# Encoder trunk: eight weight slots around norms, the last FFN step by token block, block 0 turned at other places, loads reordered at the start

## The chip, the cores and the metric

The kernel runs on one core of a Trainium2 chip. The metric is the device time of one execution in microseconds (us), taken as the median of several runs.

## The reference, cut to what matters

Two layers (`DEPTH = 2`) work on one sequence of 256 tokens with 1024 features, in fp32. `memory_cross_attention` reads 256 rows of a second input, `mem`.

```python
for l in range(DEPTH):
    x = layer_norm(ALPHA * x + 0.5 * swiglu(x, ffn1_w13[l], ffn1_w2[l]), ln_g[l, 0], ln_b[l, 0])
    h = x @ w_in[l]                                # pool channels | c_q | c_kv | k_pe
    y_mix = jnp.concatenate([pool_mixer(...), mla_mixer(...)], axis=-1) @ w_out[l]
    x = layer_norm(ALPHA * x + y_mix, ln_g[l, 1], ln_b[l, 1])
    y_mem = memory_cross_attention(x, mem, mem_wq[l], mem_wkv[l], mem_wo[l])
    x = layer_norm(ALPHA * x + y_mem, ln_g[l, 2], ln_b[l, 2])
    x = layer_norm(ALPHA * x + 0.5 * swiglu(x, ffn2_w13[l], ffn2_w2[l]), ln_g[l, 3], ln_b[l, 3])
```

`swiglu` is `(silu(x @ gate) * (x @ up)) @ w2` with an inner width of 2816.

## The kernel before

**Arithmetic.** Every matrix product is made of three fp32r matmuls: high part by high part, high by low, low by high. So every weight must be split before it is used: ScalarE casts it to the high part (L985), VectorE subtracts to get the low part (L1168). The same is done with activations.

**Weights as units.** Weights come as 366 units of 128 x 1024 (512 KB), in one fixed order. SyncE loads unit n into one of four raw buffers once VectorE has split unit n-4 (L479). ScalarE and VectorE then write it into one of six slots (`slot_hi`, `slot_lo`); a slot is free again when TensorE has passed the last matmul that reads it. A `Plan` counts TensorE's milestones ahead of time, and a table (`slot`, `last_user`, `free_after`) says which slot each unit takes. ScalarE and VectorE are in-order engines: the splits of coming units are put between their other work by `ahead(tag)`, which splits as many units as will have free slots when TensorE reaches that milestone, and by `ahead_to(n)`.

**FFN.** 11 steps (`FS`), of which 8 run in a hardware loop of 4 iterations x 2 steps. A step multiplies four units against both blocks of 128 tokens (`up`, 48 matmuls), turns the hidden values of the step before in the middle of that (`turn_hidden`, L698), and multiplies two units into the output rows (`down`, 24 matmuls). ScalarE makes the silu (L1025) and the cast of the turned values (L1030), VectorE the product with the up half (L1216) and the low part (L1221). At the end block 0's output is finished first (milestone `("y", e, 0)`), then block 1's in two halves of 512 columns (`("half y", e)`, `("y", e, 1)`).

**Norms.** There are eight, e = 0 to 7: e % 4 = 0 after the first FFN, 1 after `w_out`, 2 after the memory read, 3 after the second FFN. The last, e = 7, ends the kernel. VectorE does block 0 first: two halves of sum and statistics (L1258, L1261), variance (L1265, L1267), centre (L1272), then the scaling (L1280) after GpSimd's power (L1473); after that the same for block 1, with the splits of coming units in between. TensorE then turns the normed block (L613) in two halves, ScalarE casts it (L1018), and VectorE makes its low part (L1206); only then can the next stage read it. To have work in that time, TensorE computes one 256-column piece of the memory's keys or values (a *fill*, two units, 48 matmuls of 256 columns). Table `FILL` has one for every norm except those after the memory read and the second FFN of layer 1. After e = 0 and e = 1 block 1 is turned after the fill; after e = 2 and e = 3 it is turned inside the next FFN's first step, `up_begin`, which runs all of block 0 (24 matmuls) before block 1.

**The start.** SyncE issues in this order: identity, x block 0, x block 1, units 0 to 2, the other constants, unit 3, `mem` (1 MB), unit 4 and so on. TensorE turns x block 0, runs three units of `up_begin` for block 0, turns block 1, and turns `mem` between FFN steps 0 and 1. GpSimd computes the rope angles at once when constants and positions are there.

Names that the change touches: `SLOTS`, `STEPS`, `plan_norm`, `plan_rows`, `plan_ffn`, the slot table, `load`, `column_pair`, `fill`, `second_block`, `up_begin`, `turn_hidden`, `ahead`, `gate`, `round_hidden`, `multiply`, `split_hidden`, `norm`.

## Time and profile before

| | us |
|---|---|
| median of 3 runs (1176.31 to 1177.42) | 1177.41 |
| the profiled execution, its own time | 1177.25 |
| its span, first to last instruction | 1175.5 |

```profile
span 1175.5 us, 16505 instructions
```

The span is what the trace covers; 1.75 us lie around it. In the trace, PE is TensorE's matmuls, PEld its weight loads, DVE VectorE, ACT ScalarE, POOL GpSimd, SPq the queue that issues DMAs. L535 is the line of all matmuls of products, so stages are told apart by tiles and times.

### The profile page before, as it was taken

What the parts mean: (1) busy time and instruction counts of PE and PEld (TensorE: products, weight loads), DVE (VectorE), ACT (ScalarE), POOL (GpSimd) and SP (SyncE); (2) the same over time, 40 slices, a digit from 0 to 9 for tenths busy, and PEclk for the clock granted to TensorE, in tenths of its full rate; (3) what the DMA queues carried; (4) which work ended last, traced back from release to release, by engine and by line L of the source; (5) the groups of instructions that cost most, each with busy time, mean ns of one, the idle gap of its engine ahead of it and who ended that gap; (6) DMA issues with size and microseconds to landing.
All of it is one profiled execution on the core that took longest, in us unless ns stands there. A gap on an engine that the chain in (4) does not pass through costs nothing.

```text
span 1175.5 us, 16505 instructions
## 1 busy us (share of the span) xinstructions
PE 1123.4 (96%) x6020; PEld 968.4 (82%) x6020; DVE 717.6 (61%) x856; ACT 511.7 (44%) x670; POOL 106.1 (9%) x116
## 2 busy tenths in 40 slices
PE   5999999999999999999999999999999998999996
PEld 4888888899899888888888888879888986888884
DVE  3655555878766765555585555567768757555555
ACT  3544444346355254444444444434553524444440
POOL 5800000150100100000010000001401000000001
PEclk9999999999999999999999999999899998999998
DMA  8655666434482486666556665544335527665650
GB/s 257 208 185 181 194 192 196 140 117 157 126 268 93 126 267 189 186 182 194 162 183 211 194 188 188 181 141 144 121 111 190 185 88 221 200 188 183 192 161 36
DMA packets 162802, 203.56 MB, mean 173 GB/s; under 512 B 16928, under 2 KB 144160, under 8 KB 162752
## 3 DMA queue, kind: packets, MB, share of 16 engines
q1 hardware_dynamic: 159824, 194.22, 52.9%
q0 software_dynamic: 2928, 8.66, 2.3%
q8 instruction: 33, 0.54, 0.2%
q14 instruction: 17, 0.14, 0.0%
HBM read 201.79 MB, written 1.05 MB: 173 GB/s over the span
## 4 chain that ended last, share of the span: by engine, by line
PE 88%; DVE 7%; POOL 1%; ACT 1%; issue 1%; DMA 1%; SPq 0%; POOLq 0%; DVEq 0%
PE ps L535 84%; PE ps L698 2%; DVE st L1261 1%; DVE x L1258 1%; POOL st L1473 1%; DVE x L1280 1%; PE ps L613 1%; DVE w_lo L1168 1%; DMA raw<-in_ffn_w 1%; DVE xT L1206 0%; POOL tmp L1535 0%; DVE x L1272 0%; PE ps L796 0%; DVE v_flat L1168 0%; DVE xT L1180 0%
## 5 line engine op out<-in xcount | busy, mean ns | idle before, releaser
L1168 DVE TENSOR_TENSOR w_lo<-raw,w_hi 128x1024 fp32r<-128x1024 f32 (+2 forms) x253 | 306.9, 1221 | 170.9 <-ACT w_hi L985 170.2
L985 ACT CAST w_hi<-raw 128x1024 fp32r<-128x1024 f32 (+2 forms) x253 | 262.6, 1046 | 230.4 <-PE ps L535 201.7
L535 PE MATMUL ps<-w_hi,xT 128*128 128x512 f32 x880 | 286.4, 396 | 10.9 <-DVE w_lo L1168 9.2
L535 PEld LDWEIGHTS ps<-w_hi,xT 128*128 128x128 f32 x880 | 167.4, 190 | 46.5 <-DVE w_lo L1168 9.9
L535 PE MATMUL ps<-w_hi,mixT 128*128 128x512 f32 x704 | 202.8, 391 | 0.2
L535 PE MATMUL ps<-v_flat,xT 128*128 128x512 f32 x660 | 181.9, 397 | 4.6 <-DVE xT L1206 4.6
L535 PE MATMUL ps<-w_lo,xT 128*128 128x512 f32 x440 | 173.1, 393 | 0.0
L985 ACT CAST v_flat<-raw 128x1024 fp32r<-128x1024 f32 (+1 forms) x113 | 118.0, 1048 | 101.0 <-PE ps L535 94.3
L535 PEld LDWEIGHTS ps<-w_hi,mixT 128*128 128x128 f32 x704 | 131.2, 188 | 28.7 <-DVE mixT L1221 1.5
L535 PEld LDWEIGHTS ps<-v_flat,xT 128*128 128x128 f32 x660 | 123.6, 190 | 30.0 <-issue 4.8
L535 PE MATMUL ps<-w_lo,mixT 128*128 128x512 f32 x352 | 112.6, 390 | 0.0
L1168 DVE TENSOR_TENSOR v_flat<-raw,v_flat 128x1024 fp32r<-128x1024 f32 (+1 forms) x59 | 72.0, 1221 | 59.5 <-ACT v_flat L985 59.5
L1473 POOL TENSOR_TENSOR st<-st,cst 128x1 f32<-128x1 f32 x16 | 24.4, 1526 | 850.5 <-DVE st L1267 850.5
L535 PEld LDWEIGHTS ps<-w_lo,xT 128*128 128x128 f32 x440 | 83.7, 190 | 16.9
L535 PE MATMUL ps<-v_flat,mixT 128*128 128x512 f32 x320 | 83.7, 390 | 0.1
L1168 DVE TENSOR_TENSOR cqp<-raw,v_flat 128x1024 fp32r<-128x1024 f32 x54 | 66.6, 1233 | 22.9 <-ACT v_flat L985 22.6
L535 PEld LDWEIGHTS ps<-w_lo,mixT 128*128 128x128 f32 x352 | 66.1, 188 | 13.8
L1221 DVE TENSOR_TENSOR mixT<-ps,mixT 128x512 fp32r<-128x512 f32 x44 | 30.4, 691 | 67.2 <-ACT mixT L1030 67.2
L535 PEld LDWEIGHTS ps<-v_flat,mixT 128*128 128x128 f32 x320 | 59.9, 188 | 12.8 <-DVE mixT L1221 0.5
L1030 ACT CAST mixT<-ps 128x512 fp32r<-128x512 f32 x44 | 25.8, 587 | 90.5 <-PE ps L698 90.5
L1216 DVE TENSOR_TENSOR ev<-ps,ev 128x512 f32<-128x512 f32 x44 | 30.4, 691 | 45.3 <-ACT ev L1025 45.3
L1025 ACT ACTIVATE ev<-ps 128x512 f32<-128x512 f32 x44 | 26.3, 598 | 68.6 <-PE ps L535 68.5
(155 smaller groups left out, 1355.2 us busy)
## 6 DMA issues: line engine op xcount, KB each, us to landing
raw<-in_ffn_w SPq DMA_DIRECT2D x352, 256.0 KB, 3.0
raw<-in_ffn_w SPq DMA_DIRECT2D x88, 512.0 KB, 3.5
raw<-in_mem_wkv SPq DMA_DIRECT2D x32, 512.0 KB, 4.8
raw<-in_w_out SPq DMA_DIRECT2D x16, 512.0 KB, 3.8
raw<-in_mem_wq SPq DMA_DIRECT2D x16, 512.0 KB, 5.6
raw<-in_mem_wo SPq DMA_DIRECT2D x16, 512.0 KB, 4.5
gb<-in_ln_g POOLq DMA_DIRECT2D x8, 512.0 KB, 4.4
gb<-in_ln_b POOLq DMA_DIRECT2D x8, 512.0 KB, 5.3
```

The source lines that it names most:

```text
L535: return nc.tensor.matmul(dst, stand, move, start=start, stop=stop, skip_group_check=True)
L613: last = nc.tensor.transpose(ps[:, 4 + 2 * b + c, (k % 4) * P:(k % 4 + 1) * P], src[:, k * P:(k + 1) * P], ident)
L698: last = nc.tensor.transpose(hidden_banks(m + 2 * s)[:, b, t, :], ev[:, (f + s) % 2, b * S + t * P:b * S + (t + 1) * P], ident)
L985: nc.scalar.copy(slot_hi[slot[n]][:, 0:size], raw[:, n % RAW, 0:size]).then_inc(hi_done, 1)
L1025: nc.scalar.activation(ev[:, (f + s) % 2, :].rearrange("p (b c) -> p b c", b=TB), step_banks(m + 2 * s)[:, :, 0:S], ACT.Silu).then_inc(sil ...
L1030: nc.scalar.copy(hidden_columns(s, 0), hidden_banks(m + 2 * s)).then_inc(columns_hi, 1)
L1168: nc.vector.tensor_tensor(slot_lo[slot[n]][:, s], raw[:, n % RAW, s], slot_hi[slot[n]][:, s].bitcast(F32), ALU.subtract).then_inc(lo_done, 1)
L1216: nc.vector.tensor_tensor(h, step_banks(m + 2 * s)[:, :, S:2 * S], h, ALU.mult).then_inc(rows_ready, 1)
L1221: nc.vector.tensor_tensor(hidden_columns(s, 1), hidden_banks(m + 2 * s), hidden_columns(s, 0).bitcast(F32), ALU.subtract).then_inc(bank_fr ...
L1258: own(nc.vector.scalar_tensor_tensor(out=z, in0=ps[:, 4 + 2 * b + c, :], scalar=weight, in1=z, op0=ALU.mult, op1=ALU.add))
L1261: own(nc.vector.bn_stats(STATS[b][:, 6 * c:6 * c + 6], z))
L1473: nc.gpsimd.tensor_tensor(RSTD[b], VEPS[b], cst[:, C_HALF:C_HALF + 1], ALU.pow)\
```

## The change

- `SLOTS` is 8: two more slots lie in `qT`, which is free outside the mixing and memory stages. From the units of `win` to those before `wo` they are left out. The hardware loop of the FFN is 2 iterations x 4 steps so that slots repeat.
- `ahead` gets a cap: with eight slots it still goes no more than four units past the units done at the milestone, plus `more`; at `("y", e, 0)` `more` is 3.
- The FFN's last step is made by token block: a new `up_end` runs block 0 of all four units before block 1; silu, product, turn, cast and low part are made for each block by itself; block 0's rows take all four remaining units, and `second_block` then has four units where it had three.
- After FFNs (e % 4 = 0, 3) block 0 is turned between the two units of the fill. After `w_out` and the memory read it is turned inside `second_block`, after four of its six units; VectorE makes its low part right after block 1's first statistics.
- At the start x block 1 is loaded after unit 1; the constants and `mem` after unit 7. `up_first` runs units 0 and 1 for block 0, turns block 1, then goes on with both blocks. `mem` is turned after step 1. GpSimd starts the rope angles when TensorE has turned hidden step 1.

```diff
-SLOTS = 6
+SLOTS = 8
-STEPS = 2
+STEPS = 4
...
+            if plan["win", l]["units"] <= n < plan["wo", l]["units"]:
+                usable.remove(6)
+                usable.remove(7)
...
-                        if n == 2:
+                        if n == 1:
+                            load_x(1)
+                        if n == 2 * RAW - 1:
                             sp.dma_start(cst[:, P:C_ALL], consts[:, P:C_ALL]).then_inc(consts_landed, 16)
-                        if n == RAW - 1:
                             sp.dma_start(tmp[:, :].rearrange("p (b d) -> p b d", b=TB),
                                          a["mem"][0].rearrange("(b p) d -> p b d", p=P)).then_inc(mem_landed, 16)
...
+            def second_block(e, units, acts, turn_after=None):
                 for c in range(2):
                     for i, n in enumerate(units):
+                        if c == 1 and i == turn_after:
+                            turn(4 + 2 * e, x[:, 0, :], 0, e)
                         last = row_block(n, acts[i], 1, False, i == len(units) - 1, [c])
...
             def norm(e, l, place):
-                turn(4 + 2 * e, x[:, 0, :], 0, e)
-                fill(l, place)
+                if e % 4 in (0, 3):
+                    fill(l, place, lambda: turn(4 + 2 * e, x[:, 0, :], 0, e))
+                else:
+                    fill(l, place)
...
+                def up_first():
+                    order = [(0, 0), (1, 0), (0, 1), (1, 1), (2, 0), (2, 1), (3, 0), (3, 1)]
+                    take_bank(m + 1)
+                    for i, (j, b) in enumerate(order):
+                        if i == 2:
+                            pe.wait_ge(x_landed[1], 16)
+                            turn(1, x[:, 1, :], 1)
+                        if b == 0:
+                            unit_split(ffn_units(u, 0)[0] + j)
+                        pe.wait_ge(turned_lo[b], turned_lo_value(b, j // 2))
+                        n, last = up_block(0, j, b)
...
+                def up_end():
+                    s = FS - 1
+                    for b in range(TB):
+                        take_bank(m + 2 * s + b)
+                        for j in range(4):
+                            if b == 0:
+                                unit_split(ffn_units(u, s)[0] + j)
+                            n, last = up_block(s, j, b)
+                            if b == 0 and j == 1:
+                                turn_hidden(s - 1)
...
+                up(1)
                 if e == 0:
                     pe.wait_ge(mem_landed, 16)
                     for b in range(TB):
                         turn(2 + b, tmp[:, b * D:(b + 1) * D], b)
-                up(1)
-                if e == 0:
                     for b in range(TB):
                         pe.wait_ge(turned_lo[b], turned_lo_value(3, 1))
                 down(0)
...
+                up_end()
+                rest = [down_unit(s, t) for s in (FS - 2, FS - 1) for t in range(2)]
+                for b in range(TB):
+                    pe.wait_ge(rows_ready, hidden_value(f + FS - 1, b))
+                    reach(turn_hidden_block(FS - 1, b), ("hidden", e, FS - 1, b))
+                    pe.wait_ge(bank_free, m + 2 * FS - 2 + b)
+                    for n, act in rest[2 * b:2 * b + 2]:
+                        unit_split(n)
+                        last = row_block(n, act, 0, False, n == rest[-1][0])
...
-                while (limit < UNITS and last_user[limit] <= plan.units_by[done[tag] - 1] - 2 + more
+                limit, used = state["next"], plan.units_by[done[tag] - 1]
+                while (limit < UNITS and last_user[limit] <= used - 2 + min(more, 1) and limit <= used + 4 + more
                        and free_after[limit] <= done[tag]):
...
             def norm(e, l=None, place=None):
-                ahead(("y", e, 0), 1)
+                ahead(("y", e, 0), 3)
...
                 half_statistics(1, 0, ("half y", e))
                 if place is not None:
                     ahead_to(plan.units_by[done["y", e, 1] - 1] + 2)
+                    if e % 4 in (1, 2):
+                        turn(4 + 2 * e, xT, 0)
                 half_statistics(1, 1, ("y", e, 1))
                 variance(1)
                 center(1)
-                if place is not None:
+                if e % 4 in (0, 3) and place is not None:
                     turn(4 + 2 * e, xT, 0)
                 shift(1)
...
             own(nc.gpsimd.memset(pw[:, :, :, :], 0.0))
+            pool.wait_ge(pe_done, done["hidden", 0, 1])
             rope_angles()
```

## Rows read from the trace of the kernel before

**Rows 1.** The page: busy us of each engine (share of the span), instructions.

```profile
PE 1123.4 (96%) x6020; PEld 968.4 (82%) x6020; DVE 717.6 (61%) x856; ACT 511.7 (44%) x670; POOL 106.1 (9%) x116
```

**Rows 2.** What TensorE waited for: us in total, times, longest us.

```profile
PE ps L535 <- DVE xT L1206: 10.2, 5, 4.6
```

**Rows 3.** Chain that ended last, two FFN steps: start us, length us, what.

```profile
423.55 16.36 PE ps L535 x72
440.34 16.38 PE ps L535 x72
```

**Rows 4.** Timeline, start: start us, length, engine, line, operation [idle before <-releaser].

```profile
11.84 1.04 ACT L985 CAST w_hi<-raw 128x1024 fp32r<-128x1024 f32 x1 [0.46 <-DMA raw<-in_ffn_w]
...
12.69 0.80 PE L535 MATMUL ps<-w_hi,xT 128*128 128x512 f32 x1 [5.80 <-DVE w_lo L1168]
...
19.46 1.04 PE L613 MATMUL ps<-cst,x 128*128 128x128 f32 x8
...
20.72 1.29 DVE L1206 TENSOR_TENSOR xT<-ps,xT 128x512 fp32r<-128x512 f32 x2 [5.08 <-ACT xT L1018]
...
23.93 0.50 PE L535 MATMUL ps<-w_hi,xT 128*128 128x512 f32 x1 [3.43 <-DVE w_lo L1168]
...
32.46 1.28 ACT L1025 ACT_TABLE_LOAD   x1
...
32.50 1.91 PE L613 MATMUL ps<-cst,tmp 128*128 128x128 f32 x16
```

**Rows 5.** DMA issues: KB each, median us from issue to landing.

```profile
raw<-in_ffn_w SPq DMA_DIRECT2D x352, 256.0 KB, 3.0
```

**Rows 6.** Timeline around the norm after the first FFN of layer 0.

```profile
201.78 2.36 DVE L1168 TENSOR_TENSOR w_lo<-raw,w_hi 128x1024 fp32r<-128x1024 f32 x2 [0.18 <-ACT w_hi L985]
...
204.72 0.69 DVE L1258 SCALAR_TENSOR_TENSOR x<-ps,x 128x512 f32<-128x512 f32 x1 [0.58 <-PE ps L535]
...
210.44 1.32 PE L613 MATMUL ps<-cst,x 128*128 128x128 f32 x8 [1.68 <-DVE x L1280]
...
219.59 0.47 PE L535 MATMUL ps<-xT,w_hi 128*128 128x256 f32 x2 [1.05 <-DVE xT L1206]
```

**Rows 7.** Timeline after the output projection of layer 0, VectorE.

```profile
324.59 1.28 DVE L1206 TENSOR_TENSOR xT<-ps,xT 128x512 fp32r<-128x512 f32 x2
```

**Rows 8.** Timeline after the memory read of layer 0, VectorE, then TensorE.

```profile
389.00 0.69 DVE L1258 SCALAR_TENSOR_TENSOR x<-ps,x 128x512 f32<-128x512 f32 x1 [5.80 <-PE ps L535]
...
396.56 2.34 DVE L1168 TENSOR_TENSOR w_lo<-raw,w_hi 128x1024 fp32r<-128x1024 f32 x2
...
404.29 2.35 DVE L1168 TENSOR_TENSOR w_lo<-raw,w_hi 128x1024 fp32r<-128x1024 f32 x2
...
405.61 0.47 PE L535 MATMUL ps<-w_hi,xT 128*128 128x512 f32 x1 [1.71 <-issue]
```

**Rows 9.** Timeline after the memory read of layer 1, VectorE, then TensorE.

```profile
969.86 1.21 DVE L1168 TENSOR_TENSOR v_flat<-raw,v_flat 128x1024 fp32r<-128x1024 f32 x1
...
977.59 2.35 DVE L1168 TENSOR_TENSOR w_lo<-raw,w_hi 128x1024 fp32r<-128x1024 f32 x2
...
975.90 3.33 PE L535 MATMUL ps<-v_flat,xT 128*128 128x512 f32 x7 [4.60 <-DVE xT L1206]
...
982.35 1.04 PE L613 MATMUL ps<-cst,x 128*128 128x128 f32 x8
```

**Rows 10.** Second FFN of layer 0: VectorE timeline, then the chain after it.

```profile
598.45 1.28 DVE L1206 TENSOR_TENSOR xT<-ps,xT 128x512 fp32r<-128x512 f32 x2
...
594.97 11.35 PE ps L535 x66
```

**Rows 11.** Stretches: PE, PEld, DVE, ACT, POOL busy us (count), granted clock, DMA.

```profile
595.00:599.00 4.00, 4.00 (x23) 4.00 (x22) 3.90 (x7) 3.43 (x4) 1.52 (x1) 0.57 0.00 0
974.00:981.00 7.00, 5.10 (x13) 4.03 (x14) 5.94 (x7) 0.00 (x0) 2.63 (x3) 0.52 0.51 142
```

**Rows 12.** Timeline of the last norm, VectorE.

```profile
1160.49 0.69 DVE L1258 SCALAR_TENSOR_TENSOR x<-ps,x 128x512 f32<-128x512 f32 x1 [3.11 <-PE ps L535]
```

More of the change, by code:

```diff
@@ L160, in trunk, with plan_fill @@
     UI, ITEM, UNIT_ = ["U", "I"], ["I"], ["U"]
-    def plan_fill(l, place):
+    def plan_fill(l, place, between=()):
+        assert len(FILL[l, place]) == 1 or not between
         for part in FILL[l, place]:
-            plan.section(("kv", *part), [UNIT_, UI])
+            plan.section(("kv", *part), [UNIT_, *between, UI])
             plan.n["items"] += freed_by_fill(l, place) - 1
@@ L193, in plan_ffn @@
         assert plan.n["items"] % 2 == 0
-        marks = turned(second_turn(e)) + [ITEM] + [UNIT_] * 3 + [UI] + (turned(2) + turned(3) if e == 0 else [])
-        for s in range(1, FS):
-            marks += [UNIT_] * 2 + [[("hidden", e, s - 1)]] + [UNIT_, ["U", "I", "I"]] + [UNIT_] * (2 * (s < FS - 1))
-        plan.section(("ffn", l, w), marks + [[("hidden", e, FS - 1)], ["U"], [("y", e, 0)], [("half y", e)], ["U"], ["U"],
-                                             ["U", ("y", e, 1)]])
+        if e == 0:
+            marks = turned(1) + [UNIT_] * 3 + [["U", "I", "I"]]
+        else:
+            marks = turned(second_turn(e)) + [ITEM] + [UNIT_] * 3 + [UI]
+        for s in range(1, FS - 1):
+            marks += [UNIT_] * 2 + [[("hidden", e, s - 1)]] + [UNIT_, ["U", "I", "I"]]
+            marks += turned(2) + turned(3) if e == 0 and s == 1 else []
+            marks += [UNIT_] * 2
+        plan.section(("ffn", l, w), marks + [[("hidden", e, FS - 2)], ITEM] + [UNIT_] * 3 + [UI]
+                     + [[("hidden", e, FS - 1, b)] for b in range(TB)] + [[("y", e, 0)], [("half y", e)]]
+                     + [UNIT_] * 3 + [["U", ("y", e, 1)]])
     plan_turn(0)
@@ L257, in trunk @@
         for l in range(L):
-            if k >= 4 and latest[k] < plan["wout", l]["units"] <= n:
+            if k in (4, 5) and latest[k] < plan["wout", l]["units"] <= n:
                 after = done["item", plan["pv", l, PAIRS - 1]["items"]]
+            if k > 5 and latest[k] < plan["wo", l]["units"] <= n:
+                after = done["mscore", l, TB - 1]
         slot.append(k)
@@ L263, in trunk @@
         latest[k] = n
+    for n in range(FIRST_IN_LOOP, SLOTS + 8):
+        free_after[n] += len(turned(2) + turned(3))
     w13 = [a["ffn1_w13"], a["ffn2_w13"]]
@@ L471, in _, with load_x @@
             sp.dma_start(cst[:, 0:P], consts[:, 0:P]).then_inc(ident_landed, 16)
-            for b in range(TB):
+            def load_x(b):
                 sp.dma_start(x[:, b, :], a["x"][0, b * P:(b + 1) * P, :]).then_inc(x_landed[b], 16)
+            load_x(0)
             def load(n, parts, it=None):
@@ L571, in column_pair @@
                     reach(last, ("unit", n + half), *([("item", m)] if half else []))
+                    if between is not None and half == 0:
+                        between()
             def row_block(n, act, b, first, last_unit, halves=range(2)):
@@ L615, in turn, with fill @@
                     reach(last, ("turned", job, c))
-            def fill(l, place):
+            def fill(l, place, between=None):
                 for l, i in FILL[l, place]:
@@ L638, in fill @@
                         reach(last, ("unit", n), *([("item", m)] if half else []))
+                        if between is not None and half == 0:
+                            between()
             def norm(e, l, place):
-                turn(4 + 2 * e, x[:, 0, :], 0, e)
-                fill(l, place)
+                if e % 4 in (0, 3):
+                    fill(l, place, lambda: turn(4 + 2 * e, x[:, 0, :], 0, e))
+                else:
+                    fill(l, place)
                 if e % 4 < 2:
@@ L969, in loop_first @@
         def loop_first(l, w):
-            first = plan["ffn", l, w]["units"] + 7 + SLOTS
+            first = plan["ffn", l, w]["units"] + FIRST_IN_LOOP
             for n in range(first, first + LOOP_UNITS * (LOOPS - 1)):
@@ L1040, in ffn @@
                 gate(1)
+                if e == 0:
+                    for b in range(TB):
+                        turn(2 + b, memT, b)
                 first = loop_first(l, w)
@@ L1232, in ffn @@
                 multiply(1)
+                if e == 0:
+                    for b in range(TB):
+                        turn(2 + b, memT, b)
                 first = loop_first(l, w)
@@ L1245, in ffn @@
                 split_hidden(FS - 2)
+                ahead(("item", m + 2 * FS - 2))
+                multiply(FS - 1, b=0)
                 ahead(("item", m + 2 * FS - 1))
-                multiply(FS - 1)
-                split_hidden(FS - 1)
+                multiply(FS - 1, b=1)
+                for b in range(TB):
+                    split_hidden(FS - 1, b=b)
             def norm(e, l=None, place=None):
```

121 lines of the change are left out of this document (63 added, 58 removed).

## The prediction, made before the changed kernel ran

> **What bounds the kernel now.** I read the page first: TensorE is busy 96% of the span [rows 1]. Then the chain: one FFN step is a piece of 72 matmuls, 16.36 us (0.227 us each), and the next begins 16.79 us later [rows 3]. The 0.43 us between are its own turns of hidden values. The loops hold 36 of the 44 steps and have no slack, so nothing can be won inside them; the change keeps their work and order. What is left is idle time at the start, around the eight norms and in the mixing stage. The waits say who ends it: the low parts of turned activations 10.2 us in five waits [rows 2]. So I take stage by stage which engine is late there, VectorE or TensorE. Last, the stretches: after some gaps TensorE is granted 1.2 GHz instead of 2.4 for a while. At 595 us the mean over 4 us is 0.57, that is 3.4 us at half, and costs 1.7 us; at 974 us it is 0.52 over 7 us, and 13 matmuls take 5.10 us instead of 2.95 [rows 11].
>
> **Loop of 2 x 4 steps, cap in `ahead`.** 0. A slot's reuse is eight units back instead of six, the split order is the same, and TensorE waits for no unit in a step [rows 3]. The rope angles on GpSimd move beside FFN steps; VectorE has room there (61% busy [rows 1]).
>
> **The last FFN step by block.** Before, TensorE waits 0.25 us for the hidden low parts, and block 0's rows are followed by 18 matmuls of block 1. Afterwards 24 follow: block 0 is ready 6 x 0.227 = 1.36 us earlier plus 0.25, less about 0.1 for split turns: 1.5 us. Block 1 is ready 0.25 us earlier. `up_end` needs a unit every 1.36 us, but four are split ahead of it: no wait.
>
> **The last norm (e = 7).** VectorE starts at 1160.49 after 3.11 us idle [rows 12] and is then at work or waiting for GpSimd's power to the end; no split lies ahead of it. It starts 1.5 us earlier and so does the end. **Gain 1.5** (1.0 to 1.6).
>
> **Norms after the first FFN (e = 0, 4).** TensorE turns block 0 at 210.44 after 1.68 us idle [rows 6]; half a fill (2.9 us) will cover that. But VectorE works from 204.72 until the low part of block 1 lets TensorE on at 219.59 [rows 6], with under 1 us idle. So what counts is its start. By the slot table it splits three units ahead of the statistics instead of two. The two begin at 201.78 and take 2.36, ending 0.58 us before block 0's sum is there [rows 6]. The third adds 1.13; the cast in front of it is 0.2 us earlier: start at about 205.1, 0.4 later, although the sum is ready 1.5 us earlier. On the way back it no longer waits for the fill (0.35). **0 at both** (-1 to +0.5). TensorE's idle time is moved to one gap of about 2.5 us ahead of block 1's turn.
>
> **Norms after `w_out` (e = 1, 5).** `qT` is in use, the table has six slots, and no split moves. VectorE's line up to the low part at 324.59 [rows 7] holds the same work in another order. **0** (-0.5 to +0.5).
>
> **After the memory read, layer 0 (e = 2).** Here slots 6 and 7 are free again, so the two fill units are split in the 5.80 us in which VectorE sat idle before 389.00 [rows 8], and not at 396.56 (2.34 us) between block 1's halves [rows 8]. The turn inside the tail needs the normed block 0 at 395.8, and it is there at 395.3. It makes block 1's rows 0.9 us late, so VectorE wins 1.2 to 1.7 and not 2.3. The FFN's units are then split from 402.6, not 404.29 [rows 8], each 1.13 us. TensorE ends the fill at 403.9 and its first unit is ready at 403.8: the 1.71 us wait before 405.61 [rows 8] goes. Next late would be the units, 1.13 us apart against 1.36 needed. **Gain 1.7** (0.8 to 1.7).
>
> **After the memory read, layer 1 (e = 6), no fill.** TensorE now waits 4.60 us for block 0's low part until 975.90 [rows 9], as two splits (from 969.86) and block 1's statistics stand in front of it. After: turned in the tail at 969.1, low part at 971.4, block 1's rows done at 971.3: the FFN starts at 971.4, 4.5 us earlier. What is late next are its third and fourth unit: they stay behind block 1's scaling, which begins only 1.4 us earlier, so the split at 977.59 [rows 9] comes at 976.2 and is done at 977.4. Two units for block 0 take 2.7 us, to 974.1, then 3.3 us of wait. The third ends at 978.8 where before it ended at 982.4 [rows 9]: 3.7 us. Before, a slow stretch lay there [rows 11]; after a 3.3 us gap I expect one of 3.4 us too (1.7 us lost). **Gain 2.0** (2.0 to 3.7).
>
> **After the second FFN, layer 0 (e = 3).** VectorE again starts 0.4 us later and makes block 0's low part at 598.9 instead of 598.45, first half at 599.5 [rows 10]. TensorE gets through fill and turn by 598.3 and waits 1.3 us. Its third unit is split by 602.7; the 66 matmuls end at about 604.2, before at 594.97 + 11.35 = 606.32 [rows 10]. 1.7 of these 2.1 us are the slow stretch [rows 11] that a gap of 1.8 us had started. The remaining gap is smaller and I let it go. **Gain 2.1** (0.4 to 2.1).
>
> **The start.** Units land 1.5 us apart: a cast of 1.04 us, then 0.46 us of waiting for the next [rows 4]. x block 1 is as large as a unit, so without it unit 0 is there up to 1.5 us earlier; I take 1.3, and TensorE's first product goes from 12.69 to 11.4 [rows 4] (0 to 1.5: it may be latency, not bytes). Two units for block 0 at half clock, 5.3 us, to 16.7; then block 1's turn, and its first low part 1.95 us after the turn's start (19.46 to the middle of the pair from 20.72 [rows 4]): TensorE goes on at 18.6. 36 matmuls to 26.8, against 32.50 [rows 4] before. The 3.43 us wait for unit 3 [rows 4] is gone, since its cast no longer stands behind block 1's turn. 24 matmuls of step 1 end at 32.3; now the hidden values of step 0 must be ready. Their silu stands behind the cast of unit 8 on ScalarE, and unit 8 stands behind constants and `mem` (1.4 MB) in SyncE's queue. Unit 3 is split at 21.8, which releases unit 7; a pair of loads takes about 3.6 us (3.0 for one of its two [rows 5]), so unit 7 lands at 25.6; 1.9 MB more at 1.5 us each 0.5 MB: 30.9. Cast 1.05, table load 1.28 [rows 4], silu 0.6, product 0.7: 34.4, a stall of 2.2 us (0 to 3.5).
>
> The Trainium skill, page "ScalarE: Activation LUTs", section "What ACT_TABLE_LOAD costs", gives a drain of about 1.4 us on top of the load. This would make the stall 3.6 and the total 1.4 us later; the load's row is 1.28 us, and the silu followed it at once, so the sum doesn't take it.
>
> The rest of step 1 ends at 40.5. Then comes the turn of `mem`: before, a step ran beside its casts and low parts; now `down` needs its banks at once. Turn 1.91 [rows 4] and the last low parts make 4.1 us: 44.6. Before: 32.5 + 1.91 + 11.35 (48 matmuls and the hidden turn) = 45.7. **Gain 0.9** (-2.5 to +3).
>
> **Sum.** 0.9 + 1.7 + 2.1 + 2.0 + 1.5 = 8.2. Against it I set one new slow stretch of 1.7 us: there are new gaps of over 2 us at 32, 42, 215 and 795 us, and in this trace two gaps of 1.8 us out of some eight were followed by one. 8.2 - 1.7 = 6.5 us. The profiled execution took 1177.25, so 1170.75; the median lies 0.16 above it: **1170.8**.
>
> **Rivals.**
> 1. *The slow stretches go and no new ones come, or the silu of step 0 isn't held up.* For: fewer gaps near norms, and unit 8 may land early. Gain 8.2 + 1.7 (e = 6) or + 2.2 (start): **1166.5**. Chance 0.17.
> 2. *The gaps are only moved and each costs clock.* The new gap of 2.5 us before block 1's turn at e = 0 and 4 starts a slow stretch each time, and so does one at the start; e = 3 keeps its own. 8.2 - 3 x 1.7 - 1.7 = 1.4, to 4 us: **1174.5**. For: VectorE's line through the norm isn't shorter. Chance 0.15.
> 3. *The change doesn't do what it says*: the turn in the tail waits for the normed block (it has only 0.5 us in hand at e = 1, 2, 5 and 6) and the start gains nothing. Left: e = 7, **1176.3**. Chance 0.08.
> 4. *Slower.* The third unit split ahead of the statistics (e = 0, 3, 4) is loaded only when the unit four before it is split, about 6 us before its cast is due. A landing later than that makes the whole norm wait, as VectorE works in order. A load takes 3.0 us and more [rows 5]. From 6 us on, each further one costs 3 us over the three places. At 8.5 us it is 7.5, with slow stretches after it (3 x 1.7) 12.6 in all, against 8.2 gained: **1181**. Against: only two DMA pairs are outstanding then. Chance 0.05.
>
> **How the numbers follow.** Forecast 0.55, own range 1167.5 to 1173.8; rivals 0.17, 0.15, 0.08, 0.05. 0.2% is 2.35 us, about what can be told from no change. Faster: 0.55 + 0.17 + 0.10 of rival 2 = 0.82; same: 0.05 + 0.08 = 0.13; slower 0.05. Range 1166.0 to 1175.2: it leaves out half of rival 1's lower side, the end of rival 2, and rivals 3 and 4.
>
> **What would show it.** Steps of 16.8 us unchanged. At the norms after FFNs: three splits ahead of the statistics, no idle TensorE before block 0's turn, but one before block 1's. At e = 2 no wait for the FFN's first unit; at e = 6 the 4.6 us wait replaced by one for its third. At the start a wait for hidden step 0 at 32 us and one after the turn of `mem`. I am wrong if VectorE's line through e = 0 gets shorter or longer by over 1 us, if units aren't there in `up_end`, or if slow stretches appear inside the loops.

## The result, and the profile after

The changed kernel is slower: 1188.22 us, median of four executions (1183.75 to 1190.42), against 1176.86 (1175.04 to 1177.42) of the kernel before; ratio 1.0094, 95% interval 1.0063 to 1.0126. The forecast was 1170.8. The profiled execution of after took 1183.75 and is the quickest of the four, so the profile shows 6.1 us of span (1181.6 against 1175.5), not the whole 11.

The page of after, its busy lines (us, share of the span, instructions), against [rows 1]:

```profile
span 1181.6 us, 16536 instructions
PE 1125.3 (95%) x6020; PEld 970.4 (82%) x6020; DVE 705.1 (60%) x864; ACT 497.1 (42%) x678; POOL 106.6 (9%) x116
```

TensorE has as many matmuls as before and is busy 1.9 us longer; the other 4.2 us are idle time. The clock can be taken out another way. Executions list their span and their mean granted clock; span x clock is about the time at full clock (it also halves idle time that lies in a slow stretch, and the clock is rounded to 0.001, which is 1.2 us). I call span minus that the clock loss, and the change of the time at full clock waits. By this measure the profiled execution has 2.5 us of waits and 3.6 of clock, so the split is good to 1 or 2 us only. Means over the executions (the 26 of before were taken beside experiments 5 to 8):

| kernel (executions) | span | at full clock | clock loss |
|---|---|---|---|
| before (26) | 1174.9 | 1159.3 | 15.6 |
| after (4) | 1185.5 | 1163.6 | 21.9 |

So of 10.6 us some 4.3 are waits and 6.3 are clock, where the forecast had 8.2 gained and 1.7 lost.

Where the waits are: the starts of the first turn of hidden values in the second, third and fourth FFN, TensorE in the timeline of after (a "slow stretch" below is one in which TensorE is granted 1.2 GHz):

```profile
428.46 0.60 PE L773 MATMUL ps<-cst,ev 128*128 128x128 f32 x4
...
622.77 0.60 PE L773 MATMUL ps<-cst,ev 128*128 128x128 f32 x4
...
1003.35 0.60 PE L773 MATMUL ps<-cst,ev 128*128 128x128 f32 x4
```

| up to | before | after | stage, after minus before | forecast |
|---|---|---|---|---|
| second hidden turn of FFN 1 (start) | 56.51 | 56.91 | +0.4 | -0.9 |
| first of FFN 2 (e = 0, 1, 2) | 422.95 | 428.46 | +5.1 | -1.7 |
| first of FFN 3 (e = 3) | 619.32 | 622.77 | -2.1 | -2.1 |
| first of FFN 4 (e = 4, 5, 6) | 995.49 | 1003.35 | +4.4 | -2.0 |
| end of span (e = 7) | 1175.5 | 1181.6 | -1.8 | -1.5 |

Of the norms to which the prediction gave most of its working, e = 3, 6 and 7 came out. The loss is in the two stretches that hold a norm after an FFN, the mixing stage and the memory stage. The waits of TensorE in after (us in total, times, longest), against [rows 2]:

```profile
PE ps L568 <- DVE w_lo L1245: 7.5, 2, 4.1
PE ps L568 <- DVE xT L1283: 7.4, 6, 1.8
PE ps L650 <- DVE x L1362: 6.0, 4, 2.5
PE ps L980 <- DVE tmp L1405: 5.7, 2, 4.0
...
PE ps L773 <- DVE ev L1293: 3.0, 1, 3.0
```

The wait for turned low parts fell from 10.2 to 7.4, as meant. But the fourth line has none that answers to it before: TensorE's turn of the probabilities of the memory read (L980) waits 5.7 us for VectorE's scaling. VectorE in the timeline there, layer 1, first the kernel before, then after (start, length; L1311 and L1395 are the maxima of a block's scores, L1321 and L1405 the scaling):

```profile
930.17 1.23 DVE L1311 TENSOR_REDUCE st<-ps 128x4 f32<-128x1024 f32 x1 [1.57 <-PE ps L535]
...
933.05 1.23 DVE L1311 TENSOR_REDUCE st<-ps 128x4 f32<-128x1024 f32 x1 [1.45 <-PE ps L535]
...
934.59 1.14 DVE L1321 TENSOR_SCALAR tmp<-tmp,st 128x256 f32<-128x256 f32 x4
```

```profile
923.33 1.22 DVE L1245 TENSOR_TENSOR w_lo<-raw,w_hi 128x1024 fp32r<-128x1024 f32 x1 [0.52 <-ACT w_hi L1056]
...
933.61 1.23 DVE L1395 TENSOR_REDUCE st<-ps 128x4 f32<-128x1024 f32 x1 [1.57 <-PE ps L568]
...
937.97 2.36 DVE L1245 TENSOR_TENSOR qT<-raw,qT 128x1024 fp32r<-128x1024 f32 x2 [2.93 <-ACT qT L1056]
940.24 1.22 DVE L1245 TENSOR_TENSOR w_lo<-raw,w_hi 128x1024 fp32r<-128x1024 f32 x1
941.38 1.22 DVE L1395 TENSOR_REDUCE st<-ps 128x4 f32<-128x1024 f32 x1
...
942.91 1.14 DVE L1405 TENSOR_SCALAR tmp<-tmp,st 128x256 f32<-128x256 f32 x4
```

Before, nothing lies between the two maxima (2.88 us apart). After, three unit splits do, and they are 7.77 us apart (933.61 to 941.38). The tile names say why: two of the units go to `qT`, the two new slots. ScalarE makes their casts after the exponentials of block 0, VectorE waits 2.93 us for them, and the second block's maxima queue behind. In layer 0 it is one split (362.33) and TensorE waits 1.7 us.

These splits are missing earlier. From 905.48, just behind `wq`'s first matmul in layer 1, to the first maxima VectorE makes 11 unit splits before, the last at 925.54; from the same place (908.92) after it makes 8, the last at 923.33, and then none for 13 us. In layer 0 it makes 11 before and 10 after.

This isn't the whole loss of the profiled execution. In layer 0 two new slow stretches, 6.8 us at 219 and 3.4 us at 270 (shown further down), cost up to half their length, 5.1 us, against the 1.7 us of the new wait.

### The profile page after: what moved, and what is told of

It is laid out like the page before. It is cut to its first block, busy times and chain, and to the rows that moved or that the text cites. A ratio compares the mean times of both kernels' runs of the same rounds, so it can differ in the third digit from the quotient of the medians.

```text
span 1181.6 us, 16536 instructions
## 1 busy us (share of the span) xinstructions
PE 1125.3 (95%) x6020; PEld 970.4 (82%) x6020; DVE 705.1 (60%) x864; ACT 497.1 (42%) x678; POOL 106.6 (9%) x116
## 3 DMA queue, kind: packets, MB, share of 16 engines
HBM read 201.79 MB, written 1.05 MB: 172 GB/s over the span
## 4 chain that ended last, share of the span: by engine, by line
PE 83%; DVE 10%; ACT 2%; POOL 2%; issue 1%; DMA 1%; POOLq 0%; SPq 0%; DVEq 0%; ACTq 0%
PE ps L568 80%; PE ps L773 2%; DVE w_lo L1245 1%; DVE st L1343 1%; DMA raw<-in_ffn_w 1%; DVE x L1340 1%; POOL st L1557 1%; DVE x L1362 1%; DVE xT L1283 1%; ACT tmp L1152 1%; DVE v_flat L1245 1%; PE ps L650 0%; DVE st L1395 0%; POOL tmp L1620 0%; ACT w_hi L1056 0%
## 5 line engine op out<-in xcount | busy, mean ns | idle before, releaser
L1245 DVE TENSOR_TENSOR w_lo<-raw,w_hi 128x1024 fp32r<-128x1024 f32 (+2 forms) x202 | 240.5, 1217 | 42.3 <-ACT w_hi L1056 41.7
L568 PE MATMUL ps<-w_hi,xT 128*128 128x512 f32 x704 | 229.9, 396 | 9.8 <-DVE w_lo L1245 7.5
L1056 ACT CAST w_hi<-raw 128x1024 fp32r<-128x1024 f32 (+2 forms) x202 | 204.1, 1041 | 68.9 <-PE ps L568 39.2
L568 PE MATMUL ps<-v_flat,xT 128*128 128x512 f32 x460 | 125.1, 392 | 0.5 <-issue 0.5
L568 PE MATMUL ps<-qT,xT 128*128 128x512 f32 x504 | 121.5, 396 | 0.0
L568 PEld LDWEIGHTS ps<-qT,xT 128*128 128x128 f32 x504 | 94.9, 190 | 20.0 <-DVE qT L1245 0.4
L1056 ACT CAST v_flat<-raw 128x1024 fp32r<-128x1024 f32 x90 | 93.0, 1053 | 24.7 <-PE ps L568 17.4
L1245 DVE TENSOR_TENSOR qT<-raw,qT 128x1024 fp32r<-128x1024 f32 x74 | 89.7, 1223 | 18.8 <-ACT qT L1056 18.8
L1056 ACT CAST qT<-raw 128x1024 fp32r<-128x1024 f32 x74 | 76.7, 1052 | 12.1 <-DMA raw<-in_ffn_w 10.3
L568 PE MATMUL ps<-qT,mixT 128*128 128x512 f32 x336 | 79.8, 390 | 0.0
```

The source lines that it names most:

```text
L568: return nc.tensor.matmul(dst, stand, move, start=start, stop=stop, skip_group_check=True)
L1056: nc.scalar.copy(slot_hi[slot[n]][:, 0:size], raw[:, n % RAW, 0:size]).then_inc(hi_done, 1)
L1245: nc.vector.tensor_tensor(slot_lo[slot[n]][:, s], raw[:, n % RAW, s], slot_hi[slot[n]][:, s].bitcast(F32), ALU.subtract).then_inc(lo_done, 1)
```

## The experiments

**Theory.** The slot table gives `wo`'s first units the slots that are longest unused, which are 6 and 7. They stay barred until the second scores are made (`done["mscore", l, TB - 1]`), since `qT` is read until then. Units are split in order, so one barred slot stops the whole look-ahead during `wq`, and it is made up as soon as it may be, which is between the two softmaxes. **Rivals**: the new order at the norms after FFN 1 (turn between the fill units, third split) is at fault through the clock; the new start is.

The ratios are to the kernel before. After's own is 1.0063 to 1.0126, and the intervals of experiments 1 to 4 overlap it, so their times alone don't tell them from after; there the traces do. Experiment 5 against after, 7 against 6 and 12 against 10 are apart also in time.

**1. Another release for slots 6 and 7**

```diff
-                after = done["mscore", l, TB - 1]
+                after = done["item", plan["mpt", l, 0]["items"]]
```

> The changed kernel with one edit: the slots in qT (6 and 7) count as free after the first turned probabilities of the memory read, not already after its second scores. Theory A (the look-ahead at the second scores splits units into the freed slots ahead of the maxima, so VectorE waits for casts that stand behind the exponentials on ScalarE): the waits for tmp before the turn of probabilities, 1.9 us in layer 0 and 4.0 + 1.9 us in layer 1, fall to 0 and to the 2.0 us of the kernel before; about 6 us less than the changed kernel, so about 1178 profiled, 1182 in the median. Rival B (the softmax is late because units land late, not because of their place in the order): the waits stay, within 1 us of the changed kernel (1184 profiled, 1188 median).

Measured: 1184.87 (1183.58 to 1187.27), ratio 1.0063 (1.0046 to 1.008). TensorE and VectorE in layer 1:

```profile
952.14 2.90 PE L568 MATMUL ps<-xT,memV 128*128 128x256 f32 x12 [8.66 <-DVE xT L1257]
```

```profile
936.88 1.23 DVE L1395 TENSOR_REDUCE st<-ps 128x4 f32<-128x1024 f32 x1 [1.45 <-PE ps L568]
...
944.21 2.36 DVE L1245 TENSOR_TENSOR qT<-raw,qT 128x1024 fp32r<-128x1024 f32 x2 [0.19 <-ACT qT L1056]
946.49 2.35 DVE L1245 TENSOR_TENSOR w_lo<-raw,w_hi 128x1024 fp32r<-128x1024 f32 x2
...
951.35 1.28 DVE L1257 TENSOR_TENSOR xT<-ps,xT 128x512 fp32r<-128x512 f32 x2
```

The maxima are 2.88 us apart again and the wait in layer 0 is gone: the place was right. But the held-up units are now split in a row ahead of the low part of the turned probabilities, and TensorE waits 8.7 us for that. A later release only moves the block; the fix in the expectation was wrong.

**2. The old order at the norms after FFN 1**

```diff
-        if e % 4 in (0, 3):
+        if e % 4 == 3:
...
+            if e % 4 == 0:
+                plan_turn(4 + 2 * e)
```

(and the same in TensorE's `norm`: block 0 is turned ahead of the fill again at e = 0 and 4.)

> The changed kernel with block 0 turned before the fill again after the first FFN of each layer (e = 0 and 4), as in the kernel before. Theory A (VectorE's line sets the end, and turning later only gathers TensorE's idle time into one gap of 2.0 to 2.7 us, after which it runs at half clock for 3.4 to 6.8 us): the gap is two again, 1.8 and about 1 us; the slow stretches at 219 and 803 us go; win starts within 0.5 us of where it did; 2 to 5 us less than the changed kernel. Rival B (the slow stretches come anyway): same to 1 us.

Measured: 1187.10 (1184.31 to 1188.67), ratio 1.009 (1.0073 to 1.0107): as slow as after. TensorE's gap of 2.50 us ahead of block 1's turn became one of 2.32 ahead of block 0's, and the one ahead of `win` grew from 0.75 to 1.22; the idle time is moved, not made, by this part. Of the slow stretches at 219 and 802, which I had expected to go, one of 3.4 us at 212 is left in this trace, but there are longer ones elsewhere: 6.8 us at 328, 3.4 at 871. In the means it is 2.4 us more at full clock and 3.2 less of clock loss, too close to the scatter to read more into.

**3. `mem` one unit later in SyncE's queue**

```diff
-                        if n == 2 * RAW - 1:
+                        if n == 2 * RAW:
```

> The changed kernel with constants and mem issued after unit 8 instead of after unit 7. Theory A (the silu of step 0 stands behind the cast of unit 8, and unit 8 behind mem on the queue): the 3.15 us wait for the hidden values at 31 us falls to under 0.7 us, mem lands about 1.5 us later but is not needed before 40 us; 2.5 us less, or 4 with the slow stretch at 35 us gone. Rival B (the silu waits for something else, such as its table load): the wait stays above 2.5 us and the time is the same.

Measured: 1184.94 (1182.77 to 1190.12), ratio 1.0081 (1.005 to 1.0113). TensorE at the start, after and then this one:

```profile
34.20 0.68 PE L773 MATMUL ps<-cst,ev 128*128 128x128 f32 x4 [2.99 <-DVE ev L1293]
45.91 0.70 PE L568 MATMUL ps<-w_hi,mixT 128*128 128x512 f32 x2 [2.23 <-issue]
```

```profile
33.50 0.66 PE L773 MATMUL ps<-cst,ev 128*128 128x128 f32 x4 [1.08 <-DVE ev L1293]
44.27 1.19 PE L568 MATMUL ps<-w_hi,mixT 128*128 128x512 f32 x2 [2.87 <-issue]
```

The wait for the silu of step 0 falls from 2.99 to 1.08 (I had said under 0.7), and the first `down` matmul comes 1.6 us earlier. ScalarE's cast of unit 8 no longer waits for its load: 0.23 us, where it waited 3.79 in after and 4.53 and 4.40 in 2 and 5, which have the same start. So that stall is a load queued behind `mem`, as predicted. The trace takes something off it, though: here unit 7 comes late (its cast at 28.40, in after at 25.55; why is open), so the cast of unit 8 is only 0.7 us earlier (29.68 against 30.39), and the rest of the shorter wait is TensorE arriving 1.2 us later.

**4. The whole old start**

Edit: `load_x(1)`, constants, `mem` and its turn, `up_begin` and the rope angles as in the kernel before.

> The changed kernel with the whole start of the kernel before: both x blocks first, constants and mem early, the old order of the first step, mem turned before step 1, rope angles at once. In the traces the two starts reach the first down step at 45.6 us (before) and 45.9 us (changed). Theory A (the reordered start gives nothing in sum): within 1 us of the changed kernel. Rival B (it costs, by a slow stretch in most executions): 2 to 4 us less in the median. Rival C (the angles on GpSimd now slow VectorE inside the FFN): steps 1 to 3 of the changed kernel would be longer than 16.8 us, and 1 us or more comes back.

Measured: 1183.32 (1181.28 to 1185.99), ratio 1.0061 (1.004 to 1.0081). The first `down` matmul starts at 43.8, in after at 45.9: the new start loses where it was to gain. After was even the best of the traces with the new start: experiments 1, 2 and 5 have it too and come to that matmul at 47.4, 47.1 and 48.3, with waits of 4.1 to 4.3 us for the silu. The eight traces with the old start, the kernel before among them, lie from 43.8 to 45.6.

**5. Slots 6 and 7 barred for `wo`'s first four units**

```diff
-            if plan["win", l]["units"] <= n < plan["wo", l]["units"]:
+            if plan["win", l]["units"] <= n < plan["wo", l]["units"] + 4:
```

> The changed kernel with one edit: slots 6 and 7 stay out of use for four units more, to the fourth unit of wo. Theory A, in a new form (the first units of wo take slots 6 and 7 as the longest unused, these are blocked until the second scores, and since units are split in order the whole look-ahead stops until then and is made up between the two softmaxes): the first four units of wo are split during wq as in the kernel before; the waits for tmp are 0 in layer 0 and 2.0 us in layer 1; 6 us less than the changed kernel (1178 profiled, 1182 to 1184 median). Rival B (any two more slots that come free late do this): the waits come back at the fifth and sixth unit of wo, above 3 us in layer 1.

Measured: 1179.67 (1174.28 to 1180.99, ten executions), ratio 1.0016 (1.0 to 1.0031): 8.5 us less than after. No wait of L980 on L1405 is left, VectorE makes 11 splits ahead of the maxima in each layer as in the kernel before, and TensorE in layer 1 has only the wait that the kernel before has too (1.75 us there):

```profile
946.90 1.67 PE L568 MATMUL ps<-xT,memV 128*128 128x256 f32 x12 [1.76 <-DVE xT L1257]
```

This one line of the slot table was the larger part of the 11.4 us by which after is slower than before.

**6. The same, with the old start** (edits of 4 and 5)

> The changed kernel with the edit of soft2 and the start of the kernel before (startold). If the two costs are independent, they add: startold gave 4.9 us less in the median and soft2 is to give 6: 1177 in the median, 1174 profiled, about the kernel before. If the slow stretches are what costs and they come at random, less: 1180.

Measured: 1175.21 (1172.84 to 1177.65, ten), ratio 0.9988 (0.9975 to 1.0002): 4.5 us less than 5, about as much as the old start gave alone (4.9), so the two costs add. In the means 3.2 of it are at full clock and 0.2 clock.

**7. No third split ahead of the statistics at e = 0 and 4** (on top of 6)

```diff
-                ahead(("y", e, 0), 3)
+                ahead(("y", e, 0), 2 if e % 4 == 0 else 3)
```

> soft2_start with two units instead of three split ahead of the statistics of the norms e = 0 and 4. Theory C (the third split delays VectorE's line through these norms): statistics start at once when block 0's sum is there or after the second split, about 1.1 us earlier, and win's first product 0.6 to 1.1 us earlier at both norms: 2 us less than soft2_start. Rival: the third split's time is only moved behind the norm and win waits for its second unit: same.

Measured: 1170.88 (1170.39 to 1176.03, nine), ratio 0.9958 (0.9943 to 0.9974). VectorE ahead of the first sum at e = 0, kernel of 6 and then of 7:

```profile
202.69 1.22 DVE L1239 TENSOR_TENSOR cqp<-raw,v_flat 128x1024 fp32r<-128x1024 f32 x1
203.83 0.69 DVE L1334 SCALAR_TENSOR_TENSOR x<-ps,x 128x512 f32<-128x512 f32 x1
```

```profile
201.43 1.22 DVE L1239 TENSOR_TENSOR v_flat<-raw,v_flat 128x1024 fp32r<-128x1024 f32 x1
202.56 0.68 DVE L1334 SCALAR_TENSOR_TENSOR x<-ps,x 128x512 f32<-128x512 f32 x1
```

The sum starts 1.3 us earlier (0.2 of it from the start of the kernel) without any idle time before it: it had queued behind the third split. TensorE's gap ahead of block 1's turn falls from 2.50 to 1.37. The two norms save 1.6 us at full clock in the means; the other 1.9 are clock. I had expected 2 in all.

**8. As 7, with block 0 turned ahead of the fill at e = 0 and 4** (edit of 2)

> mix_between with block 0 turned before the fill at e = 0 and 4, as in the kernel before. Theory D (one gap of 2.7 us is followed by a slow stretch more surely than gaps of 1.8 and 1 us): the stretch of half clock after win's start is gone or half as long, 1.5 to 3 us less than mix_between. Rival (norm0 showed the same number of slow microseconds, only elsewhere): same within 1 us.

Measured: 1170.95 (1168.04 to 1172.44, six), ratio 0.9948 (0.9928 to 0.9967): no difference to 7. The gaps are 1.19 us ahead of block 0's turn and 1.05 ahead of `win`, in place of 1.37 ahead of block 1's and 0.83. With the split gone, where block 0 is turned doesn't matter.

**9. Block 0's low part back in its place at e = 1 and 5** (on top of 7)

```diff
-                    if e % 4 in (1, 2):
+                    if e % 4 == 2:
                         turn(4 + 2 * e, xT, 0)
...
-                if e % 4 in (0, 3) and place is not None:
+                if e % 4 != 2 and place is not None:
                     turn(4 + 2 * e, xT, 0)
```

> mix_between with VectorE making the low part of block 0 at e = 1 and 5 after block 1's centre again, as in the kernel before, while TensorE still turns it in the tail. Theory F (that 1.2 us of work used to cover GpSimd's power, 1.54 us; moved away, VectorE waits 0.52 us for the power and TensorE 0.65 us before block 1's turn): both waits go, 0.5 us less at each of the two norms, 1 us in all: 1170 in the median. Rival: TensorE gains the 0.65 us there and waits it out at the next step: same.

Measured: 1169.05 (1165.09 to 1170.49), ratio 0.9926 (0.99 to 0.9952). VectorE at e = 1, kernel of 7 and then of 9:

```profile
319.44 1.27 DVE L1348 SCALAR_TENSOR_TENSOR x<-x,st,gb 128x1024 f32<-128x1024 f32 x1
321.24 1.41 DVE L1356 SCALAR_TENSOR_TENSOR x<-x,st,gb 128x512 f32<-128x512 f32 x2 [0.52 <-POOL st L1551]
```

```profile
319.19 1.28 DVE L1348 SCALAR_TENSOR_TENSOR x<-x,st,gb 128x1024 f32<-128x1024 f32 x1
320.38 1.28 DVE L1277 TENSOR_TENSOR xT<-ps,xT 128x512 fp32r<-128x512 f32 x2
321.58 1.40 DVE L1356 SCALAR_TENSOR_TENSOR x<-x,st,gb 128x512 f32<-128x512 f32 x2
```

The shift needs GpSimd's power. With only the centring (1.27 us) in between VectorE waits 0.52 for it; with the low part in between it doesn't. TensorE's wait of 0.5 us ahead of block 1's turn is gone at both places. The interval of the time overlaps that of 7; at full clock the means differ by 0.8 us.

**10. A third split under the power at e = 2 and 6** (on top of 9)

```diff
                 center(1)
...
+                if e % 4 == 2:
+                    ahead_to(state["next"] + 1)
                 shift(1)
```

> cover1, and at e = 2 and 6 VectorE splits one more unit between block 1's centre and its scaling. Theory G (at e = 6 TensorE stands 3.6 us before the third unit of the FFN's first step, which is split behind the scaling): that wait falls to about 1.8 us, and the 0.52 us wait for the power is covered; 1.5 to 2 us less than cover1, up to 3.5 with the slow stretch after it gone. Rival: the scaling of block 1 comes 0.6 us later and TensorE waits for its turn instead: less than 0.5 us.

Measured: 1163.72 (1163.59 to 1164.79), ratio 0.9891 (0.9874 to 0.9909). TensorE at e = 6 now waits 1.5 us for its third unit (3.5 in after), but now also 2.2 us for the first hidden values, where after, 9 and the kernel before don't wait:

```profile
967.13 1.69 PE L562 MATMUL ps<-v_flat,xT 128*128 128x512 f32 x6 [1.53 <-DVE v_flat L1239]
984.35 0.66 PE L769 MATMUL ps<-cst,ev 128*128 128x128 f32 x4 [2.18 <-DVE ev L1287]
```

So what the third unit gains is waited out later, and at full clock it gains nothing over 9 (1154.9 against 1154.3), where I had expected 1.5 to 2 us. Its 5.3 us are all clock: the mean granted clock of its four executions is 0.993 to 0.995, of 9 it was 0.988 to 0.993. The shorter gap at e = 6 explains only part of that: in the traces one slow stretch of 3.4 us goes there (973 in 9), which is worth 1.7 us, but others at 325, 840 and 864 are gone too, where the edit changes nothing. Why the clock held in all four executions stays open.

**11. Half of the new start** (on top of 10): x block 1 after unit 1 and `up_first` as in after, but constants after unit 2, `mem` after unit 3 and turned ahead of step 1, rope angles at once.

> cover12 with half of the changed start: x block 1 loaded after unit 1 and up_first (two units for block 0, turn, then both blocks), but constants after unit 2, mem after unit 3 and turned before step 1, as in the kernel before. Theory H (of the start, moving x and not waiting for the fourth unit helps by 2 to 4 us; what costs is mem behind unit 7, which holds up the silu of step 0, and its turn right before down): the first down step begins at 42 to 44 us instead of 45.2, 1.5 to 3 us less than cover12. Rival (the start is bound by the rate of the loads, so that nothing before 45 us counts): same.

Measured: 1161.17 (1157.86 to 1163.26), ratio 0.9863 (0.9836 to 0.989): the quickest of all, 1.4% under the kernel before. TensorE at the start:

```profile
11.10 0.80 PE L566 MATMUL ps<-w_hi,xT 128*128 128x512 f32 x1 [4.42 <-DVE w_lo L1244]
...
18.41 0.51 PE L566 MATMUL ps<-w_hi,xT 128*128 128x512 f32 x1 [0.96 <-DVE xT L1282]
26.74 1.91 PE L648 MATMUL ps<-cst,tmp 128*128 128x128 f32 x16
33.94 0.60 PE L771 MATMUL ps<-cst,ev 128*128 128x128 f32 x4
```

Against 10 the interval overlaps, but the times at full clock don't (1149.9 to 1151.8 against 1154.4 to 1155.7). The hidden turn has no idle time before it, and the first `down` matmul starts at 39.9 against 44.4 in 10 and 45.6 in the kernel before. That is earlier than the 42 to 44 that I had expected.

**12. The old last FFN step in the kernel of 10**: both blocks together again, the same units ahead of the norms.

> cover12 with the last FFN step of the kernel before in all four FFNs (both blocks together; block 0's sum is followed by 18 matmuls instead of 24), with as many units split ahead of the norms. Theory I (the block order gives 1.4 us at the end of the kernel and 0.3 to 1 us at e = 0, 3 and 4, where VectorE's line starts earlier): 2.5 to 4 us more than cover12. Rival (only the end gains, the other norms wait for the splits anyway): 1.4 us more.

Measured: 1170.91 (1168.88 to 1171.6), ratio 0.9947 (0.9927 to 0.9967): 7.2 us slower than 10, where 2.5 to 4 had been expected. In the means it is 2.7 us at full clock and 3.8 of clock. So in this kernel the step by block is worth more than the waits that it saves.

Means of span, time at full clock and clock loss of all of them (before, in the three groups of executions: 1158.9, 1159.3 and 1159.3 at full clock):

| kernel | span | at full clock | clock loss |
|---|---|---|---|
| 1 release | 1183.0 | 1164.7 | 18.3 |
| 2 old order | 1184.6 | 1166.0 | 18.7 |
| 3 `mem` later | 1183.5 | 1161.9 | 21.6 |
| 4 old start | 1181.3 | 1161.9 | 19.5 |
| 5 slots barred | 1176.6 | 1159.9 | 16.7 |
| 6 and old start | 1173.2 | 1156.7 | 16.5 |
| 7 two splits | 1169.7 | 1155.1 | 14.6 |
| 8 turn first | 1168.5 | 1155.7 | 12.9 |
| 9 cover at e = 1, 5 | 1166.2 | 1154.3 | 12.0 |
| 10 cover at e = 2, 6 | 1161.8 | 1154.9 | 7.0 |
| 11 half start | 1158.7 | 1150.9 | 7.8 |
| 12 old last step | 1168.4 | 1157.6 | 10.8 |

## Why the prediction was wrong, step by step

**"The change keeps their work and order"; idle time is left "in the mixing stage", but no term for it; at e = 1 and 5 "the table has six slots, and no split moves".** This is the step that failed. The loops did keep 16.8 us a step. But the table has six slots only up to `wo`: the first units of `wo` take the new slots, and the prediction never asked until when these are barred. Splits did move, three in layer 1 and one in layer 0, to between the two softmaxes. This cost TensorE waits of 1.7 us in layer 0 and 4.0 in layer 1 (after's two waits of L980), and clock besides: experiment 5, which changes this alone, takes 8.5 us off the median; the means of spans fall by 8.9, of which 3.7 are waits and 5.2 clock. My rivals did not hold it either: rival 4 looked for lateness of a load, and it was lateness of a slot.

It is half of the miss. The forecast was 1170.8 and the median 1188.2, 17.4 us more, and with the slot table mended the kernel (5) is at 1179.7, still no quicker than before. The other terms that failed are the start (4.5 us, 6 against 5), the third split at e = 0 and 4 (4.3 us, 7 against 6) and the order of work at e = 1 and 5 (1.8 us, 9 against 7). Kernel 9, with all four put right, takes 1169.1. Each of these prices holds clock as well as waits.

**The forecast's arithmetic.** 1170.75 + 0.16 is 1170.9 and not 1170.8; by the same sums rival 1 is at 1167.0 to 1167.5 and not 1166.5, rival 3 at 1175.9 and not 1176.3, rival 4 at 1181.8 and not 1181. None of this matters beside 17 us.

**Loop.** Right: hidden turns 16.8 us apart, and in this trace no slow stretch starts inside the loops.

**Last norm, 1.5.** Right: 1.8 in the trace. VectorE's first sum starts after 1.92 us of idle time where [rows 12] had 3.11.

```profile
1166.64 0.69 DVE L1340 SCALAR_TENSOR_TENSOR x<-ps,x 128x512 f32<-128x512 f32 x1 [1.92 <-PE ps L568]
```

**e = 0, 4: 0.** Right for VectorE: [rows 6] has the sum at 204.72 and `win` going on at 219.59, after has:

```profile
205.41 0.68 DVE L1340 SCALAR_TENSOR_TENSOR x<-ps,x 128x512 f32<-128x512 f32 x1
...
217.91 1.40 PE L650 MATMUL ps<-cst,x 128*128 128x128 f32 x8 [2.50 <-DVE x L1362]
220.06 2.26 PE L568 MATMUL ps<-xT,v_flat 128*128 128x256 f32 x9 [0.75 <-DVE xT L1283]
```

The sum is 0.7 later and the end 0.5, but 0.4 of both come from the start (56.91 against 56.51 in the table above). The norm itself has its sum 0.3 later (0.4 was said) and its end 0.1. The gap of 2.5 us ahead of block 1's turn is there as predicted, and so is its price: a slow stretch follows at 219 in layer 0 and at 802 in layer 1. The stretches of after (PE, PEld, DVE, ACT, POOL busy us, clock, DMA):

```profile
219.00:226.00 7.00, 6.25 (x31) 5.97 (x29) 6.13 (x7) 4.72 (x7) 0.00 (x0) 0.51 0.35 101
270.00:274.00 4.00, 4.00 (x21) 4.00 (x21) 3.31 (x6) 3.69 (x5) 0.00 (x0) 0.57 0.13 47
...
802.00:807.00 5.00, 4.29 (x23) 4.32 (x24) 4.74 (x6) 4.29 (x5) 0.00 (x0) 0.66 0.22 59
946.00:953.00 7.00, 5.26 (x24) 4.89 (x25) 4.21 (x6) 2.65 (x5) 0.00 (x0) 0.51 0.52 150
987.00:991.00 4.00, 3.71 (x14) 3.03 (x15) 1.37 (x2) 0.14 (x1) 0.51 (x1) 0.57 0.75 217
```

The kernel before has, besides [rows 11], slow stretches of 3.4 us at 25 and 325 and one of 6.8 at 844; after has ones of 3.4 at 35 and 331 as well and none at 595 and 844. Up to the last norm this is 23.8 us at half clock before and 30.6 after, 3.4 us of time. New gaps that cost clock are rival 2's mechanism, and together with the waits it happened. The 0.4 us for the third split hid what it cost: 7 showed that leaving it out brings the first sum 1.1 us earlier, the start taken off, because the block order had made the sum ready that early. The split ate the whole gain of the new last step at these norms.

**e = 1, 5: 0, "the same work in another order".** Wrong by some 0.6 us each. The order is what covered GpSimd's power (9). The low part that [rows 7] have at 324.59 comes at 329.47, 4.9 later; 0.6 of it arises here (from the second gap of the mixing stage to `wq`'s first matmul kernel 7, at full clock there, takes 60.5 us and the kernel before 59.9), most of the rest in the slow stretches at 219 and 270.

**e = 2: 1.7.** From VectorE's first sum to the FFN's first matmul [rows 8] have 389.00 to 405.61, 16.6 us; after has 395.82 to 411.10, 15.3. Gain 1.3, and 0.5 us of wait left. The mechanism was right.

**e = 6: 2.0.** Right. From the first sum (962.30 before, 972.07 after) to the first hidden turn 1.9 us were gained. The wait for the third unit, said to be 3.3 us with a slow stretch behind it, is there:

```profile
986.02 2.35 DVE L1245 TENSOR_TENSOR w_lo<-raw,w_hi 128x1024 fp32r<-128x1024 f32 x2
...
987.29 0.80 PE L568 MATMUL ps<-w_hi,xT 128*128 128x512 f32 x1 [3.46 <-DVE w_lo L1245]
```

**e = 3: 2.1.** Right to 0.1: the stage is 2.1 shorter, the remaining wait is 1.32 us (1.3 was said) and no slow stretch follows it, unlike [rows 11]. In 1.7 of the 2.1 us there is luck, since whether a stretch follows a gap differs between traces (see the last section).

**Start: 0.9.** The sign was wrong: 0.3 us later at the first `down` matmul (45.91 against 45.62), 1.2 off, and in the three other traces with this start 1.5 to 2.7 us later. The range, -2.5 to +3, held the profiled execution, but the worst of the four is just outside it. The first product came at 10.93 (11.4 said) and the hidden turn at 34.20 (34.4 said). The two units for block 0 took 4.4 us and not 5.3, so TensorE stood at the hidden turn earlier, and the stall was 3.0 and not 2.2 (4.1 to 4.3 in the other three). The sum for unit 8's landing has a slip as well: 25.6 and 3.8 times 1.5 give 31.3, not 30.9; its cast started at 30.39. The turn of `mem` came at 41.77 and not 40.5, with a slow stretch of 3.4 us at 35 before it, which the term left out; the 4.1 us from there to the `down` matmul are as said. The stall's cause was right (3). That `mem` is better turned under a step's cover fits 11, which moved the constants and `mem` in the queue too, so it isn't shown alone.

```profile
30.39 1.05 ACT L1056 CAST w_hi<-raw 128x1024 fp32r<-128x1024 f32 x1 [3.79 <-DMA raw<-in_ffn_w]
31.45 1.28 ACT L1096 ACT_TABLE_LOAD   x1
32.75 0.60 ACT L1096 ACTIVATE ev<-ps 128x512 f32<-128x512 f32 x1
```

The silu again starts 0.02 us after the load's end. The Trainium skill, page "ScalarE: Activation LUTs", section "What ACT_TABLE_LOAD costs", would have put a drain of about 1.4 us there; this trace doesn't show it, neither behind the load nor ahead of it, where the cast ends at 31.44.

**Clock: one stretch, 1.7.** Mis-sized: 6.3 us more in the means than before. The profiled execution, being the quickest, shows only 3.4 to 3.6 of it.

## What to carry to other kernels

When buffers are added to an in-order look-ahead, list for every unit which buffer it gets and when this is released: one that is released late stops all units behind it, and the work comes back in a burst at the worst place. Ahead of moving an instruction, see what stands between the request to another engine and its use; the work in another order is not the same work. Price a change in waits and in clock apart: here the clock loss moved by as much as the waits and not in step with them (5.2 us beside 3.7 of waits in 5, 5.0 beside none in 10, and 3.2 less beside 2.4 more in 2), and a single profiled execution told little of it.

## What the runs showed of the hardware

Gaps of 1 to 3 us can be followed by TensorE at 1.2 GHz: after's 2.50 us at 217.9 by 6.8 us of it, gaps of 1.04 and 1.66 us at 265 and 269 by 3.4 us at 270. It isn't certain, and the length isn't either. The kernel before has the last two gaps at 262 and 266, and no stretch followed them; it has them again at 842 and 845, with 6.8 us at half clock from 844, and there after has none (847 and 850). After's gap of 2.49 us at 800.6 was followed by 3.4 us where the one at 217.9 had 6.8. Four executions of after span 1181.6 to 1188.3 us at mean clocks of 0.984 to 0.979, while the time at full clock stays within 1162.7 to 1165.2. So most of the spread is the clock's. Kernel 10 lies within 1.2 us in four executions at 0.993 to 0.995, but kernel 11, whose gaps in the trace are none longer, spreads over 5.4 again; what decides in one execution stays open.
